# Ahead of the second FFN of a hybrid decoder layer: GpSimd takes over one weight split, VectorE sums the mixer's output tiles

## The reference, cut to what matters

```python
def swiglu(h, w_gu, w_down):
    g, u = jnp.split(h @ w_gu, 2, axis=-1)
    return (jax.nn.silu(g) * u) @ w_down

x = layer_norm(ALPHA*x + 0.5*(1+g1)*swiglu(mod(x; s1, sc1), w_gu1, w_down1), ln_g[0], ln_b[0])
# the mixer: a pooling branch and a gated linear recurrence, then an output projection
x = layer_norm(ALPHA*x + (1+g2)*(concat(y_pool, y_lru) @ w_out),             ln_g[1], ln_b[1])
x = layer_norm(ALPHA*x + 0.5*(1+g3)*swiglu(mod(x; s3, sc3), w_gu2, w_down2), ln_g[2], ln_b[2])
```

## Time and profile before

| | |
|---|---|
| median of three runs | 1003.29 us |
| the profiled execution: its time | 1004.19 us |
| the profiled execution: span from first to last instruction | 1002.4 us |
| PE busy | 983.5 us (98%) |
| DVE busy | 611.8 us (61%) |
| ACT busy | 450.6 us (45%) |
| POOL busy | 103.6 us (10%) |
| read from memory | 233 MB, 234 GB/s over the span |

### The profile page before, as it was taken

One profiled execution on the slowest core, in us unless ns is written; L12 is line 12 of the kernel. 1 busy time (PEld: TensorE's weight loads), 2 busy tenths in 40 slices (PEclk: granted clock), 3 DMA queues, 4 the chain that ended last, 5 costly groups with the idle time before them and its releaser, 6 DMA issues. The chain is left out here.

```text
span 1002.4 us, 19823 instructions
## 1 busy us (share of the span) xinstructions
PE 983.5 (98%) x8624; PEld 935.1 (93%) x8624; DVE 611.8 (61%) x929; ACT 450.6 (45%) x546; POOL 103.6 (10%) x160
## 2 busy tenths in 40 slices
PE   6999999999999999999999999999999999999996
PEld 5899999998988999999989999999898899999996
DVE  2466454567897656454577545455689866555564
ACT  2354344335684544443354544433468454444341
POOL 1140000000310610000006000000030043000000
PEclk9999999999999999999999999999999999999998
DMA  9999986984739897958577796858553967664731
GB/s 329 300 264 337 310 265 237 329 301 160 292 103 337 254 274 196 312 172 318 186 233 232 207 332 172 315 181 322 171 218 130 311 183 201 190 193 157 226 111 44
DMA packets 261361, 235.67 MB, mean 235 GB/s; under 512 B 7647, under 2 KB 239193, under 8 KB 261258
## 3 DMA queue, kind: packets, MB, share of 16 engines
q1 hardware_dynamic: 258896, 230.71, 72.6%
q0 software_dynamic: 2080, 3.58, 1.2%
q10 hardware_dynamic: 298, 0.10, 0.0%
HBM read 233.11 MB, written 1.78 MB: 234 GB/s over the span
## 5 line engine op out<-in xcount | busy, mean ns | idle before, releaser
L524 PE MATMUL bank<-m_hi,w_hi 128*128 128x264 f32 x1664 | 475.6, 286 | 2.2 <-DVE w_lo L1090 1.5
L525 PE MATMUL bank<-m_lo,w_hi 128*128 128x264 f32 x1664 | 471.9, 284 | 0.0
L526 PE MATMUL bank<-m_hi,w_lo 128*128 128x264 f32 x1664 | 471.3, 283 | 0.0
L1090 DVE TENSOR_TENSOR w_lo<-raw,w_hi 128x2048 fp32r<-128x2048 f32 (+3 forms) x154 | 333.9, 2169 | 204.5 <-ACT w_hi L863 203.9
L863 ACT ACTIVATE w_hi<-raw 128x2048 fp32r<-128x2048 f32 (+2 forms) x152 | 272.3, 1793 | 173.9 <-PE bank L526 158.7
L524 PEld LDWEIGHTS bank<-m_hi,w_hi 128*128 128x128 f32 x1664 | 313.3, 188 | 10.9 <-issue 8.4
L525 PEld LDWEIGHTS bank<-m_lo,w_hi 128*128 128x128 f32 x1664 | 313.6, 188 | 0.1
L526 PEld LDWEIGHTS bank<-m_hi,w_lo 128*128 128x128 f32 x1664 | 312.2, 188 | 0.0
L524 PE MATMUL bank<-h_hi,w_hi 128*128 128x264 f32 x672 | 193.2, 288 | 0.0
L526 PE MATMUL bank<-h_hi,w_lo 128*128 128x264 f32 x672 | 190.9, 284 | 0.0
L525 PE MATMUL bank<-h_lo,w_hi 128*128 128x264 f32 x672 | 190.8, 284 | 0.0
(11 more groups left out here) (230 smaller groups left out, 529.4 us busy)
## 6 DMA issues: line engine op xcount, KB each, us to landing
raw<-in_ffn_wgu_dram SPq DMA_DIRECT2D x168, 512.0 KB, 5.3
ada_raw<-in_w_ada_dram SPq DMA_DIRECT2D x72, 1024.0 KB, 9.2
raw<-in_ffn_wdown_dram SPq DMA_DIRECT2D x48, 512.0 KB, 3.6
raw<-in_ffn_wdown_dram SPq DMA_DIRECT2D x48, 384.0 KB, 4.3
raw<-in_w_in_dram SPq DMA_DIRECT2D x24, 512.0 KB, 4.6
raw<-in_w_out_dram SPq DMA_DIRECT2D x16, 384.0 KB, 6.3
raw<-in_w_out_dram SPq DMA_DIRECT2D x8, 256.0 KB, 6.9
x_rows<-in_x_prompt_dram SPq DMA_DIRECT2D x1, 1024.0 KB
```

Of the source, the lines that this page charges most:

```text
L524: pe.matmul(out, hi, r_hi, start=start, stop=False)
L525: pe.matmul(out, hi, r_lo, start=False, stop=False)
L526: mm = pe.matmul(out, lo, r_hi, start=False, stop=stop)
L1090: dve.tensor_tensor(w_lo[:, g % SLOTS, 0:n], raw[:, g % SLOTS, 0:n], w_hi[:, g % SLOTS, 0:n].bitcast(F32), ALU.subtract).then_inc(lo_split, 1)
```

## The change

In both layers:

- POOL splits unit 45 of the layer (the first of the second FFN) in one instruction over 128 x 2048 elements. It stands in POOL's queue ahead of `finish_x(l, 1)` and waits for `hi_split` of the unit and for `lo_split` of the unit before it. DVE's `split(g0 + 6)` is gone.
- DVE takes out tiles 2 to 6 one at a time as they are finished, and adds each to `zsum` as it comes. After tile 6 it counts a new semaphore, `mixed_sum`.
- PE waits for `mixed_sum` and multiplies `zsum` once; tiles 4, 5 and 6 are not multiplied by themselves any more. Tile 7 still is.
- `coefficients(l, 2)` moves from behind the subtraction of the mean to a place between the sum of tiles 0 and 1 and the eviction of tile 2.
- In `normalise` a wait for `lo_split` of unit 45 stands ahead of the second half of unit 46's split, to keep the counter in order.

```diff
+            def split(g):
+
+                pool.wait_ge(hi_split, g + 1)
+                ready(pool, g - 1)
+                pool.tensor_tensor(w_lo[:, g % SLOTS], raw[:, g % SLOTS], w_hi[:, g % SLOTS].bitcast(F32), ALU.subtract)\
+                    .then_inc(lo_split, 1)
...
                     load_heads(l + 1)
+                split(l * UNITS + UP[1])
                 finish_x(l, 1)
...
             def mixer_stats(l):
                 n, s = l * 3 + 1, l * 15 + 5
-                pe.wait_ge(evicted, n * DT + 5)
+                pe.wait_ge(mixed_sum, l + 1)
                 stat(bank[MEAN], mean_w, zsum[:], True, False)
-                stat(bank[MEAN], mean_w, z[:, 4], False, False)
-                pe.wait_ge(evicted, n * DT + 7)
-                stat(bank[MEAN], mean_w, z[:, 5], False, False)
-                stat(bank[MEAN], mean_w, z[:, 6], False, False)
                 pe.wait_ge(evicted, n * DT + 8)
                 stat(bank[MEAN], mean_w, z[:, 7], False, True).then_inc(mean_out, 1)
...
                     if i == 1 and m == 3:
+                        ready(dve, l * UNITS + UP[1])
                         split_half(l * UNITS + UP[1] + 1, 1).then_inc(lo_split, 1)
...
                 residuals((0, 1))
                 dve.wait_ge(evicted, n * DT + 2)
                 own.did(dve.tensor_tensor(zsum[:], z[:, 0], z[:, 1], ALU.add))
-                split(g0 + 6)
-                residuals((2, 3))
-                dve.wait_ge(evicted, n * DT + 4)
-                for m in (2, 3):
-                    own.then(dve.tensor_tensor(zsum[:], zsum[:], z[:, m], ALU.add))
-                residuals((4,))
-                residuals((5, 6))
+                coefficients(l, 2)
+                for m in range(2, 7):
+                    residuals((m,))
+                    dve.wait_ge(evicted, n * DT + m + 1)
+                    if m < 6:
+                        own.did(dve.tensor_tensor(zsum[:], zsum[:], z[:, m], ALU.add))
+                    else:
+                        dve.tensor_tensor(zsum[:], zsum[:], z[:, m], ALU.add).then_inc(mixed_sum, 1)
                 residuals((7,))
                 dve.wait_ge(mean_out, n + 1)
                 dve.wait_ge(evicted, (n + 1) * DT)
...
-                coefficients(l, 2)
                 split_half(g0 + 7, 0).then_inc(half_split, 1)
```

More of the change, by code:

```diff
@@ L303, in trunk @@
         vector_steps = sem("vector_steps")
+        mixed_sum = sem("mixed_sum")
         gu_view = [w.rearrange("l (k p) (h f c) -> l h f p k c", p=P, h=2, c=P) for w in (ffn1_wgu, ffn2_wgu)]
```

## The result

The changed kernel took 1013.93 us (median of 4 runs, 1012.51 to 1014.38), the kernel before 1003.33 us beside it. The ratio is 1.0102 with a 95% interval of 1.009 to 1.0114: slower by 1%, some 10.6 us by the medians. The forecast was 1013.5 us, within 1009.0 to 1018.5.

A forecast was written before the change was run, and what follows sets the result against it. PE bounds the kernel, busy 983.5 of 1002.4 us. A mean 3.9 us later per layer (7.8) and the clock at 1.2 per layer (2.4) add 10.2 to the median 1003.29: 1013.5 us, range 1009.0 to 1018.5.

The forecast's parts named there:

- POOL's instruction: POOL's split of unit 45 over 128 x 2048 elements, from 307.9 in layer 0: 4.6 us, between 3.8 and 5.8.
- The block: Tile 2's L1500, reading two SBUF tiles, waits from 308.1 until POOL's split ends at 312.5: 4.4 us.
- The reading by which only 0.6 us ever falls on DVE: At tile 2's L1500, only the longest extra seen, 0.62 us, falls on DVE; the change then comes out even.
- no block: Rival at tile 2's L1500: POOL gives DVE the reads in between; 1.0 us faster in all, 1002.3; chance 0.10.
- Where it struck: Layer 0: POOL starts 0.2 us after ACT's 307.72; the held instruction is L1500 of tile 2, at 308.1.
- The pace of a tile: DVE's eviction one by one after the block: 1.33 us a tile, tile 6's add ending at 318.4.
- The clock: PE stands still about 5 us before the sum and its clock falls: 1.2 us a layer, 2.4 in all.
- its own signs of being wrong: Wrong if L1500 takes 0.17 us, POOL's split is much under 3.8, or the clock's share is far from 2.4.
- the work that comes first: PE's work after the gap, tile 7's sum (0.44) and turned rows (1.05): 1.5 us, used to price the clock.
- The parts at nothing: Place of coefficients, unit 48's load, the wait added in normalise, and finish_x behind POOL's split: no cost.
- The removed sums: Three PE sums, six instructions, 1.3 us: part of PE's wait from 313.3 to 318.4, bringing nothing by themselves.
- the load of unit 48: It waits for POOL's split, 312.5 instead of 310.0, but SP is held at unit 47 until 317.30: no cost.

The follow-up runs named there:

- the eight pieces: The change, with POOL's split of unit 45 in 8 instructions of 256 elements at the same place: 1009.71 us, ratio 1.0066.
- late split: The change, with POOL's split of unit 45 held until tile 7 is away: 1002.05 us, ratio 0.9989.
- fills: The late split, with three POOL memsets of the unit's low part, 128 x 2048 each, in the split's old place: 1002.61 us, ratio 0.9993.
- the change with PE kept busy: The change, with 21 throwaway matmuls of 128 columns in PE's gap ahead of the wait for mixed_sum: 1010.59 us.
- kernels with PE kept busy: Throwaway matmuls in PE's gap, added to the change (1010.59 us) and to the change with unit 45's split given back to DVE (1007.09 us).
- before, split late: The kernel before with POOL's split of unit 45 alone, held until tile 7 is away: 1002.79 us, ratio 0.9995.
- the split back on DVE: The change, with its split of unit 45 given back to DVE between coefficients and tile 2: 1008.47 us, ratio 1.0056.

## Why the prediction was right, step by step

**POOL's instruction.** Taken at 4.6 us between 3.8 and 5.8; it took 4.60 and 4.62. Scaling the rest by size after taking off DVE's fixed part (0.18 us) was the right reading of the row. That POOL's fixed part is DVE's was assumed; the eight pieces bear it out, 0.73 us forecast for 256 elements by these two terms and 0.738 measured (median).

**The block.** Shown. The held instruction ended within 0.1 us of POOL's in both layers, the pieces shorten the wait, reads hold and writes don't, and a late split frees DVE. The rule of the Trainium skill that I had weighed (SBUF — State Buffer, section Who interferes with whom: exclusive for the whole instruction, and only against a POOL instruction that reads) now has rows for both halves: 4.08 to 4.68 us of waiting, and none beside 5.55 us of fills. The reading by which only 0.6 us ever falls on DVE is refuted.

Two readings of rows in this step were wrong, and cost it certainty, not microseconds. That no row showed a long exclusion was not so: the trace of the kernel before has it with the engines the other way round. A POOL instruction that usually takes 0.62 us began beside DVE's split and took 2.67, to 0.36 us behind the split's end; in the same way two of L455 in layer 0 took 2.8 us (the longest of its row):

```profile
337.19 0.62 POOL L458 TENSOR_SCALAR x<-x,pT 128x264 f32<-128x264 f32 x1
...
338.64 2.67 POOL L458 TENSOR_SCALAR x<-x,pT 128x264 f32<-128x264 f32 x1
```

```profile
338.63 2.32 DVE L1090 TENSOR_TENSOR w_lo<-raw,w_hi 128x2048 fp32r<-128x2048 f32 x1 [1.25 <-ACT w_hi L863]
```

So the chance of 0.10 for no block was too high. And of the 84 of L1295 only 12 ran beside an instruction with which POOL computes, in all of them L458, which reads one tile. That a DVE instruction with one operand in PSUM isn't held by a POOL instruction that reads two tiles was first shown by the late split, whose subtraction took its 2.61 us.

**Where it struck.** Wrong in layer 0. POOL started 0.08 us behind ACT, not 0.2, and ACT itself was 2.16 us behind the first eviction (306.64 from 304.48) where it had been 2.69. So POOL caught the last coefficient instruction, before any of tile 2. That cost 0.85 us: tile 7 was away 7.05 us after the block's end in layer 0 (318.39 from 311.34), but 6.20 in layer 1 and in the change with PE kept busy, where the block struck the samples' add in both layers. POOL's earlier start gave most of it back: from the first eviction tile 7 was away after 13.91 us in layer 0 (318.39 from 304.48), and after 13.64 in the kernel with PE kept busy (318.59 from 304.95). That the two nearly cancel is luck.

**The pace of a tile.** Mis-sized: 1.33 us forecast, 1.26 measured (311.46 to 312.72). With POOL's exact time this makes the block and the eviction 7.20 us in two layers where the forecast had 7.8.

**The clock.** That it would fall was right; its price was mis-sized, 3.5 us (10.66 - 7.20) against the 2.4 forecast: by its own signs of being wrong (a share far from 2.4 us) the part nearest to a miss. I had set it by the work that comes first. But the clock fell 5.2 and 3.7 us after PE had stopped (318.1 from 312.88, 802.8 from 799.10), not 1.0 us after, as at the end of the run, and it was low for 3.4 us in layer 0 and 6.8 in layer 1, over part of the squares too. The two errors, -0.6 and +1.1, nearly cancel; that 1013.5 came closer than its parts is luck.

**The parts at nothing.** The removed sums and the load of unit 48 behaved as said: SP was held in the issue ahead of it from 306.57 to 316.01, past POOL's end at 311.34, and beside the new gap PE's waits are those of before.

**Where the loss lies,** by differences of the stretch; for the second and third lines of kernels with PE kept busy, so that the clock is out of them:

| part | us in two layers |
|---|---|
| new sum and order, with no split on DVE's path (late split) | -1.11 |
| a 2.3 us split on DVE ahead of tile 2, evictions and adds one by one behind it | +4.31 |
| POOL's 4.6 us in its place | +4.00 |
| the clock | +3.46 |

The second line is the one I had not priced by itself. The kernel before had the same 2.29 us split in nearly the same place, and to take it off DVE's path brought only 0.35 us there (before, split late). In the new order the same split on DVE costs 4.3 us, and the kernel with it is 3.2 us longer than before at a full clock. My reading is that before, PE made the sums of tiles 4 to 6 while DVE caught up in pairs, and that taking those sums from PE left DVE with no slack. This is not shown: eviction by single tiles and the moved sums came together in every run with an early split. The order of these lines matters: in the old order POOL's early split costs 2.9 us against its late place (2.52 + 0.35), in the new one the 8.3 of lines two and three.

## What to carry to other kernels

Work moved to GpSimd isn't off VectorE's path if both read two operands in SBUF at that time: one long GpSimd instruction then holds VectorE's next two-operand add to its end, even one of 0.17 us. Ask where in time its reads fall, and put them beside VectorE work that reads PSUM or behind a wait of VectorE's own; the same instruction moved by 8 us turned +1.0% into -0.1%. And count a gap in TensorE's work twice, once for its length and once for the clock: at this place each gap of 2.79 to 4.89 us was followed by a fall, and none of 0.28 to 0.86 us was.

## What the runs showed of the hardware that I had not expected

The clock could fall after PE had started again: in the change's layer 0 at about 318.1, when PE had resumed at 317.77 (in layer 1 at about 802.8, before PE resumed at 803.46). With the split back on DVE and with the eight pieces it fell 1.0 to 1.4 us after PE had resumed, in both layers. It came back after 3.4 us in layer 0 but only after 6.8 in layer 1, though both layers ran the same instructions; in the two other kernels it was low for 3.4 us each time. And the exclusion works both ways: the pieces of POOL's split took 0.73 to 0.74 us, but of eight two took 0.93 or so, beside DVE's adds. That all eight took 6.05 us where one instruction took 4.62 comes for the most part from the fixed time of each.
